# Latent attention and MLP on one core: first loads in finer pieces, low rotary passes on 64 rows, and the order of the attention pairs around them

## The reference

```python
def mla_mixer(x, w_in, q_norm, kv_norm, w_uq, w_ukv, w_o):
    h = x @ w_in                                   # 2048 -> 512 (q), 512 (kv), 64 (rotary key)
    cq, ckv = rms_norm(h[..., :512], q_norm), rms_norm(h[..., 512:1024], kv_norm)
    q = (cq @ w_uq).reshape(B, S, 16, 128 + 64)    # 128 plain and 64 rotary columns
    kv = (ckv @ w_ukv).reshape(B, S, 16, 128 + 128)
    q_rope, k_rope = apply_rope(q[..., 128:]), apply_rope(h[..., 1024:])   # one rotary key for all heads
    o = causal_softmax_attention(concat(q_nope, q_rope), concat(k_nope, k_rope), v, 192 ** -0.5)
    return o @ w_o

h = layer_norm(ALPHA * x + mla_mixer(x, ...))
out = layer_norm(ALPHA * h + jnp.square(jax.nn.relu(h @ w1)) @ w2)
```

## Time and profile before

| | us |
|---|---|
| median of three runs | 1808.7 |
| profiled execution | 1811.48 |
| its span, first to last instruction | 1809.5 |
| TensorE busy | 1784.0 |
| VectorE busy | 1533.6 |
| ScalarE busy | 942.4 |
| GpSimd busy | 175.0 |

### The profile page before, as it was taken

The page is one execution under the profiler, slowest core; times in us unless marked ns, Lnnn a source line. Parts: engine busy times, 40 slices in busy tenths (PEclk is TensorE's granted clock), DMA queues, the critical chain, the costliest instruction groups (busy, mean ns, idle before and its releaser), DMA issues.

```text
span 1809.5 us, 26333 instructions
## 1 busy us (share of the span) xinstructions
PE 1784.0 (99%) x9980; PEld 1555.3 (86%) x9980; DVE 1533.6 (85%) x1866; ACT 942.4 (52%) x1189; POOL 175.0 (10%) x98
## 2 busy tenths in 40 slices
PE   9999999999999999999999999999999999999997
PEld 7878988977889999999999999988888888888886
DVE  3167777699999999999999999989889999989986
ACT  4256666553456666666666666644333334333442
POOL 2333323000020000000000000000011111100003
PEclk9999999999999999999999999999999999999999
DMA  6222433598224766566556656678475474754832
GB/s 236 94 74 90 139 119 119 200 342 301 104 81 167 235 211 202 175 206 212 191 186 209 213 175 200 238 307 328 153 273 199 181 287 158 275 200 163 308 121 93
DMA packets 131588, 351.23 MB, mean 194 GB/s; under 512 B 7616, under 2 KB 80192, under 8 KB 113088
## 3 DMA queue, kind: packets, MB, share of 16 engines
q1 hardware_dynamic: 57120, 275.14, 41.4%
q10 hardware_dynamic: 74400, 75.26, 13.3%
HBM read 268.06 MB, written 82.31 MB: 194 GB/s over the span
## 4 chain that ended last, share of the span: by engine, by line
PE 91%; DVE 6%; issue 1%; DMA 1%; ACT 1%; ACTq 0%; DVEq 0%
PE bank L2234 24%; PE bank L2238 24%; PE bank L2239 24%; PE bank L2571 12%; PE bank L2575 6%; PE bank L2417 1%; DVE w_lo L1600 1%; DMA o_b<-out_weights 1%; PE bank L2409 0%; PE bank L2407 0%; DVE small L1555 0%; DMA first_raw<-weights 0%; DVE small L1710 0%; DVE up_both L1806 0%; PE bank L2332 0%
## 5 line engine op out<-in xcount | busy, mean ns | idle before, releaser
L1299 ACT ACTIVATE w_hi<-d_b 128x1024 fp32r<-128x1024 f32 x180 | 189.5, 1061 | 299.0 <-PE bank L2239 240.4
L2234 PE MATMUL bank<-w_hi,down_act 128*128 128x512 f32 x864 | 336.7, 390 | 0.4 <-issue 0.4
L2238 PE MATMUL bank<-w_lo,down_act 128*128 128x512 f32 x864 | 336.2, 389 | 0.0
L2239 PE MATMUL bank<-w_hi,down_act 128*128 128x512 f32 x864 | 336.2, 389 | 0.0
L2571 PE MATMUL bank<-up_both,w_hi 128*128 128x512 f32 x896 | 321.1, 397 | 0.0
L2234 PE MATMUL bank<-up_both,w_hi 128*128 128x256 f32 x912 | 258.2, 283 | 1.2 <-issue 1.0
L2238 PE MATMUL bank<-up_both,w_hi 128*128 128x256 f32 x912 | 258.0, 283 | 0.0
L2239 PE MATMUL bank<-up_both,w_lo 128*128 128x256 f32 x912 | 257.9, 283 | 0.0
L1970 DVE TENSOR_TENSOR w_lo<-d_b,w_hi 128x1024 fp32r<-128x1024 f32 x180 | 215.0, 1228 | 22.8 <-ACT w_hi L1299 22.8
L2575 PE MATMUL bank<-up_both,w_lo 128*128 128x256 f32 x896 | 233.3, 281 | 0.0
L1819 DVE TENSOR_TENSOR w_lo<-up_b,w_hi 128x1024 fp32r<-128x1024 f32 x180 | 217.1, 1219 | 10.1 <-ACT w_hi L1044 10.1
(11 more groups left out here) (233 smaller groups left out, 3217.5 us busy)
## 6 DMA issues: line engine op xcount, KB each, us to landing
up_b<-up_weights SPq DMA_DIRECT2D x128, 512.0 KB, 4.5
d_b<-down_weights SPq DMA_DIRECT2D x64, 1024.0 KB, 5.4
down_act<-acts_kept SPq DMA_DIRECT2D x56, 1024.0 KB, 5.3
acts_kept<-h_hi ACTq DMA_DIRECT2D x32, 896.0 KB, 4.2
acts_kept<-h_lo ACTq DMA_DIRECT2D x32, 896.0 KB, 5.5
raw<-weights SPq DMA_DIRECT2D x44, 512.0 KB, 3.3
o_b<-out_weights SPq DMA_DIRECT2D x16, 1024.0 KB, 8.5
o_act<-o_kept SPq DMA_DIRECT2D x13, 1024.0 KB, 9.4
```

The lines of the kernel that those rows point to most:

```text
L1299: act.activation(w_hi[:, DOWN_SLOT[n], :], source[:, ab, :], ACT.Copy).then_inc(down_hi, 1)
L2234: first_pass = pe.matmul(out_, a_hi, b_hi, start=start, stop=False, skip_group_check=more)
L2238: pe.matmul(out_, a_hi, b_lo, start=False, stop=False, skip_group_check=more)
L2239: return pe.matmul(out_, a_lo, b_hi, start=False, stop=stop, skip_group_check=more)
```

## The change

Sizes and loads. `kr_lo` has one copy of the low key in each half of the partitions instead of two half-empty ones, and is no longer filled with zeros. Of blocks 0 and 2, columns 0 to 255 and 256 to 511 come in pieces of 128 KB each on ScalarE's queue, and the last 512 columns in one piece each (block 0 on ScalarE's queue, block 2 on SyncE's, after x tile 3):

```diff
-            load_rest(1, 4)
             load_x_tile(3, 4)
+            sp.dma_start(first_raw[:, 1, 2 * FIRST_COLS:HB], w[2, :, 2 * FIRST_COLS:HB]).then_inc(first_loaded[11], 16)
...
-            for j in range(2):
-                act.dma_start(first_raw[:, j, 0:FIRST_COLS], w[2 * j, :, 0:FIRST_COLS]).then_inc(first_loaded[2 * j], 16)
-            act.dma_start(first_raw[:, 0, FIRST_COLS:HB], w[0, :, FIRST_COLS:HB]).then_inc(first_loaded[3], 16)
-
-            def first_weights(j):
-                act.wait_ge(*((first_loaded[0], 16), (first_loaded[2], 32))[j])
-                act.activation(w_hi[:, j, 0:FIRST_COLS], first_raw[:, j, 0:FIRST_COLS], ACT.Copy).then_inc(first_hi, 1)
+            for n in range(4):
+                j, cols = n % 2, slice(FIRST_COLS * (n // 2), FIRST_COLS * (n // 2) + FIRST_COLS)
+                act.dma_start(first_raw[:, j, cols], w[2 * j, :, cols]).then_inc(first_loaded[n + 1 if n else 0], 16)
+            act.dma_start(first_raw[:, 0, 2 * FIRST_COLS:HB], w[0, :, 2 * FIRST_COLS:HB]).then_inc(first_loaded[11], 16)
+
+            def first_weights(n):
+
+                j, cols = n % 2, slice(FIRST_COLS * (n // 2), FIRST_COLS * (n // 2) + FIRST_COLS)
+                act.wait_ge(first_loaded[n + 1 if n else 0], 32 if n else 16)
+                act.activation(w_hi[:, j, cols], first_raw[:, j, cols], ACT.Copy).then_inc(first_hi, 1)
```

The splits on ScalarE and VectorE follow: pieces 0 to 3 go ahead of the x tiles k = 0 to 3, the two remaining halves ahead of k = 4 and 5. On TensorE each of the three matmuls of k = 0 to 3 waits only for the parts that it reads:

```diff
+            def opening_product(j, k):
+
+
+                cols, n = slice(P * k, P * k + P), 2 * (k // 2) + j
+                pe.wait_ge(first_hi, n + 1)
+                pe.wait_ge(x_hi_made, k + 1)
+                pe.matmul(bank[:, j, :], w_hi[:, j, cols], act_hi[:, k, :], start=k == 0, stop=False)
+                pe.wait_ge(first_lo, n + 1)
+                pe.matmul(bank[:, j, :], w_lo[:, j, cols], act_hi[:, k, :], start=False, stop=False)
+                pe.wait_ge(x_split, k + 1)
+                pe.matmul(bank[:, j, :], w_hi[:, j, cols], act_lo[:, k, :], start=False, stop=False)
...
+            for k in range(4):
+                for j in range(2):
+                    opening_product(j, k)
+            for g in range(2, KD // 4):
```

Scores. The low rotary passes of both heads run together after all other passes, each on the 64 partitions of its head:

```diff
+                    product(score_block(h, t), q_hi[:, h, q], q_lo[:, h, q], k_hi[:, h, keys], k_lo[:, h, keys], t != 2, False, t == 2)
+
+                    pe.matmul(score_block(h, t), qr[:, h, q], kr_hi[:, keys], start=False, stop=False,
+                              skip_group_check=t == 2)
+
+            def score_lows():
+
+
+                for t in range(TT):
+                    q, keys = slice(P * t, P * t + P), slice(0, P * (t + 1))
+                    for half, h in zip(halves, range(2)):
+                        last = pe.matmul(score_block(h, t), qr[half, h, q], kr_lo[half, keys], start=False, stop=True,
+                                         skip_group_check=t == 2, tile_position=(64 * h, 0))
+                        if t == TT - 1:
+                            last.then_inc(scored, 1)
```

```diff
             root_of(1)
+            key_cross()
             weights(HB_QKV + 2)
-            key_cross()
-            weights(HB_QKV + 3)
             key_swap()
             latent_his(1)
+            weights(HB_QKV + 3)
...
-            def rope_query(pair, stream=True):
-                if stream:
-                    weights(HB_QKV + QKV_HB, pair)
+            def rope_query(pair):
                 rope_swap(pair + 1, rope_bank(pair))
 
-            def rope_query_hi(pair):
+            def rope_query_hi(pair, stream=True):
                 act.wait_ge(rope_rotated, pair + 2)
                 for half, h in zip(halves, range(2)):
                     last = act.activation(qr[half, h, :], rot[half, :], ACT.Copy)
                 last.then_inc(rope_hi, 1)
+                if stream:
+                    weights(HB_QKV + QKV_HB, pair)
...
+                if is_first(pair):
+                    act.activation(root[:, 0:1], ones[:, 0:1], ACT.Exp)
...
+                if behind:
+                    head_parts_lo(pair - 1)
                 maxima(pair, 0)
+                if ahead:
+                    query(pair + 1, 0)
                 maxima(pair, 1)
                 normalise(pair, 0)
                 if ahead:
-                    query(pair + 1, 0)
-                else:
-                    head_parts_lo(pair - 1)
+                    query(pair + 1, 1)
```

More of the change, by code:

```diff
@@ L187, in mla_mlp_program @@
         halves = (slice(0, 64), slice(64, 128))
-        kr_hi, kr_lo = sb("kr_hi", [P, S], f32r), sb("kr_lo", [P, 2, S], f32r)
-        place[0] += 2 * KB
+        kr_hi, kr_lo = sb("kr_hi", [P, S], f32r), sb("kr_lo", [P, S], f32r)
+        place[0] += 4 * KB
         v_hi, v_lo = sb("v_hi", [P, TT, 2 * VDIM], f32r), sb("v_lo", [P, TT, 2 * VDIM], f32r)
@@ L306, in score_diagonal @@
             return pairs.rearrange("p o (i n) -> p o i n", i=2)[:, :, :, 0:P]
-        first_loaded = [sem(f"first_loaded{g}") for g in range(11)]
+        first_loaded = [sem(f"first_loaded{g}") for g in range(12)]
         first_hi, first_lo = sem("first_hi"), sem("first_lo")
@@ L953, in attention @@
                     store_heads(pair - 1, 0)
+                if ahead:
+                    query(pair + 1, 0)
                 exps(pair, 0)
                 if ahead:
-                    query(pair + 1, 0)
+                    query(pair + 1, 1)
                 exps(pair, 1)
                 if ahead:
-                    query(pair + 1, 1)
-                    rope_query(pair + 1, stream)
+                    rope_query(pair + 1)
                 else:
@@ L965, in attention @@
                     key(pair + 1, 0)
-                    rope_query_hi(pair + 1)
+                    rope_query_hi(pair + 1, stream)
                 else:
@@ L1511, in key_rope_lo @@
             def key_rope_lo():
-                for h in range(2):
-                    last = dve.memset(kr_lo[64 - 64 * h:128 - 64 * h, h, :].bitcast(f32), 0.0)
-                last.then_inc(ones_made, 1)
                 dve.wait_ge(rope_hi, 1)
-                dve.wait_ge(ones_made, 2)
-                for half, h in zip(halves, range(2)):
-                    last = dve.tensor_tensor(kr_lo[half, h, :], rot[halves[0], :], kr_hi[halves[0], :].bitcast(f32), ALU.subtract)
+                for half in halves:
+                    last = dve.tensor_tensor(kr_lo[half, :], rot[halves[0], :], kr_hi[halves[0], :].bitcast(f32), ALU.subtract)
                 last.then_inc(rope_split, 1)
@@ L1648, in attention @@
                 if ahead:
-                    query(pair + 1, 0)
-                else:
-                    head_parts_lo(pair - 1)
+                    query(pair + 1, 1)
                 normalise(pair, 1)
                 if ahead:
-                    query(pair + 1, 1)
-                    if behind:
-                        head_parts_lo(pair - 1)
                     rope_query(pair + 1)
@@ L2294, in _ @@
                 pe.matmul(bank[:, 7, 0:P], ones[:, :], ones[:, :], start=True, stop=True)
-            for g in range(KD // 4):
+            for k in range(4):
+                for j in range(2):
+                    opening_product(j, k)
+            for g in range(2, KD // 4):
                 for j in range(2):
@@ L2403, in scores @@
                     q, keys = slice(P * t, P * t + P), slice(0, P * (t + 1))
-                    dst = score_bank(h)[:, SCORE_AT[t]:SCORE_AT[t] + P * (t + 1)]
-                    product(dst, q_hi[:, h, q], q_lo[:, h, q], k_hi[:, h, keys], k_lo[:, h, keys], True, False)
-                    pe.matmul(dst, qr[:, h, q], kr_hi[:, keys], start=False, stop=False)
-                    last = pe.matmul(dst, qr[:, h, q], kr_lo[:, h, keys], start=False, stop=True)
-                last.then_inc(scored, 1)
+                    product(score_block(h, t), q_hi[:, h, q], q_lo[:, h, q], k_hi[:, h, keys], k_lo[:, h, keys], t != 2, False, t == 2)
[9 more added lines that the diff above has]
+                            last.then_inc(scored, 1)
             def transpose_probs(pair, h):
@@ L2461, in attention @@
                 scores(pair, 1)
+                score_lows()
                 if ahead:
```

35 lines of the change are left out of this document (17 added, 18 removed).

## The result

The changed kernel takes 1820.34 us (median of 6 runs, 1819.84 to 1822.68), the kernel before 1808.74 beside it. The ratio is 1.0066, 95% interval 1.0053 to 1.0079. The forecast was 1805.4, in a range of 1802.5 to 1809.2, with a chance of 0.05 for slower. It was wrong in direction and size.

A forecast was written before the change was run, and what follows sets the result against it. TensorE, busy 1784.0 of 1809.5 us, was taken to bound the kernel. Opening -3.4, pair 0 0.0, pairs 1 to 6 -1.1, last pair +1.2 sum to -3.3: 1805.4 us from 1808.7, range 1802.5 to 1809.2.

The forecast's parts named there:

- The step that failed: Pairs: ScalarE waits for a weight load; head copies behind it are needed 1.9 us later, so no loss was counted.
- part 2: Pairs 1 to 6: low rotary passes on 64 rows and new order, 30.66 + L per pair, -1.1 us in all.
- The prediction's own sign of being wrong: Pairs less than 31.2 or more than 32.0, a further wait at head products, or pair 0 over 1 us off.
- Part 1, the opening: First stage: smaller pieces let x tile 3 come earlier, k=8 at 18.0 instead of 21.5; -3.4 us.
- rival A: Opening: the clock falls again in the gaps left, 1.5 us less is won, 1806.9; chance 0.27.
- L: Time of a pair's eight low rotary passes on 64 rows, switches included: 0.95 us, ends 0.84 and 2.8.
- eight loads one behind the other: Low rotary passes: loads costing by columns would make all eight load-bound, L near 1.05, the sum 0.6 us worse.
- with a margin of 0.1: Pairs: head 1's low probabilities are made at 26.6 us after the start, when TensorE arrives, so no wait.
- Part 3: Before and in pair 0: starts at 130.7 instead of 129.99, pair 1 at 163.1; 0.0 us, between -0.7 and +0.7.
- Part 4, the last pair: Last pair: no query tiles cover the later maxima, transposes start 2.2 later; +1.2 us (0 to +2).
- Slower: Whole kernel: a time above 1812.3 us, chance 0.05, made up of D and a little of another rival.
- D: Low rotary passes: weight loads not pulled ahead, L = 2.8, +10.0 in pairs 1 to 6, 1816.5; chance 0.04.

The follow-up runs named there:

- e3: Changed kernel with SyncE's first 4 MB of output projection loads held until pair 4's stores have landed too; 1809.30 us, ratio 0.9999.
- e2_store_early: Changed kernel with the store of o_lo issued directly behind ScalarE's second exponentials instead of behind the second key's weight blocks; 1810.01 us, ratio 1.0004.
- b1: Kernel before with only the opening's change (pieces, waits and `opening_product` of the first stage); 1807.32 us, ratio 0.9989.
- c3: c2 with, in the last pair, each head's low rotary passes directly behind that head's scores; 1807.31 us, ratio 0.9992.
- second profile of before: Kernel before, unchanged, profiled in one further execution; 1808.01 us, span 1806.2.
- c2: c1 with VectorE's low half of the query's rotary part behind head 1's low probabilities and the second key, in every pair; 1808.69 us, ratio 1.0002.
- c4: c3 with weight blocks 18 and 19 back in their old places ahead of the key's crossing and swap; 1805.35 us, ratio 0.9983.
- b2: b1 plus the low rotary passes on 64 rows behind both heads' scores, with ScalarE's and VectorE's order of before; 1820.65 us, ratio 1.0064.
- c1: e2_store_early with, in the last pair alone, VectorE's split of the previous pair's output back between the two normalisations; 1809.12 us, ratio 1.0005.

## Why the prediction was wrong

**The step that failed** stands in part 2: "ScalarE also waits for a weight load there, because the buffer is released later; behind it stand head copies that the next scores need 1.9 us later." The wait was seen; what is queued behind it was counted one short. Behind the block stands also the DMA issue of `store_heads(pair - 1, 1)`. By itself that is a wait of 0.45 us on ScalarE (e3). In pair 5 alone it puts the store into the 4 MB of SyncE, and the next pair waits for it: the rounding of the output, which stands at the head of ScalarE's order as before, and behind it the split, which the change had just put at the head of VectorE's. I had worked out one pair and multiplied by six; the pair in which another queue starts something new was the one to work out. Pair 6: +9.95, of which some 1.6 is the lower clock after the standstill (eight matmuls in 3.47, at 0.2275 they take 1.82). All three experiments that part the two transfers bring pair 6 to 31.7. The prediction's own sign of being wrong, a pair of more than 32.0, shows here. Without this step the result would still have missed the forecast: e2_store_early, which takes it away, has 1810.01, 4.6 more than forecast.

**Part 1, the opening (-3.4).** Against the first profile even -3.9: k=8 starts at 17.65 (18.0 forecast), the gaps left were 0.20 and 0.18, and the clock stayed at 1.00. The course of the opening was right, and rival A did not come. But it was measured against a single execution that ran 2.8 above the median, and I carried that distance to the result as if it lay outside the change. It lay in it: in the other two profiles of before k=8 starts at 19.13 and 19.17 instead of 21.56, without the half clock of the earlier trace rows and with x tile 3 copied 0.75 earlier. The term is worth 1.45 by the traces and 1.6 by b1's medians.

**Part 2, pairs 1 to 6 (-1.1).** L is 0.92 with the step into it, 0.95 forecast. The Trainium skill (TensorE: Matmul & The Clock Gate, LDWEIGHTS) has a weight load cost by its columns, not its rows, and the trace agrees: a load's record in pair 1 is 182 to 188 ns on 64 rows (`kr_lo`, changed kernel) and 187 to 192 on 128 (`kr_hi`, before). What the prediction made of it, eight loads one behind the other, is not so: in the changed kernel's trace the first loads of the two heads start at 164.841 and 164.844, and four passes (c3) take 0.83 where eight take 0.84. The Trainium skill (TensorEngine Tiling (Array Packing), Key Properties) has independent tiles and a drain at each switch of mode, which agrees with both numbers; that the remainder is drain no run here isolates. What was mis-sized is the waits. In pair 3, against the second profile of before, the first transposes start 0.17 late relative to the products ahead of them (0.13 forecast) and take 0.07 more, and the products of both heads take 3.97 instead of 3.77 (forecast none, "with a margin of 0.1"). So pairs take 31.88 where 31.6 was said. The last was the hold of GpSimd on qr, and c2 takes it away. The Trainium skill (SBUF — State Buffer; SBUF: two separate sides) says that a VectorE operation with two SBUF inputs and a GpSimd operation that reads SBUF lock each other out: qr is such a one, pt_lo has one of its two from PSUM, and the numbers of e2 and c2 agree.

**Part 3 (0.0).** The forecast was pair 0 starting 0.7 later and lasting 32.4 (130.7 to 163.1). Instead it starts unchanged: from the key's rotary tile to pair 0 the kernel before and the changed one both take 30.32 to 30.33. c4 and b2, without the zero fill and with the two blocks in their old places, take 29.07. So leaving out the fill is worth 1.25 with the blocks in their old places, and the late blocks ate exactly that, which is luck; the hold on the rotation was foreseen, that the two cancel was hidden in the sum of 0.0. Pair 0 itself is 0.5 to 0.65 longer, not shorter. The changed kernel's profile has the lower clock there (four matmuls of 0.63), but that is not the cause: in e3_loads_later the clock stays up and pair 0 takes 33.58. TensorE waits there for the bank of the values, which the kernel before doesn't:

```profile
133.79 0.50 PE L2235 MATMUL bank<-mid_hi,w_hi 128*128 128x512 f32 x1 [1.37 <-DVE v_lo L1525]
```

Which move of the new order brings this wait, no run isolates.

**Part 4, the last pair (+1.2).** +2.3. The transposes did start 2.2 later, as worked out (13.0 after the pair's start, give 10.8), but I took some of it to be made up; 2.3 stayed. The joint end of the scores is most of the cause: b2, with the old order, has the last product at 20.10 as c2 has, and c3 takes 1.5 off. The split's place is a little of it (0.27, c1), and so is the clock: c1 and c2 run the same program in the last pair and wait 2.31 ahead of the transposes, but c1 has the last product at 20.48 and c2 at 20.10. The six us around it, c1 from 363 and c2 from 362 (granted clock third from the end):

```profile
363.00:369.00 6.00, 5.65 (x28) 4.93 (x29) 5.96 (x10) 3.44 (x8) 0.00 (x0) 0.72 0.90 340
```

```profile
362.00:368.00 6.00, 4.66 (x29) 3.75 (x30) 5.96 (x11) 4.19 (x9) 0.00 (x0) 1.00 0.98 377
```

The changed kernel's profile has the lower clock there too (0.57 on the mean from 373 to 377).

**The chances.** Slower had 0.05, nearly all of it on one mechanism (D), which did not occur. A move of instructions on two engines and their queues deserved more for the chain not looked at.

## What to carry to other kernels

When an instruction that can wait is moved, list what its engine issues behind it, DMA issues above all, and for each who waits for its landing. Then look for the one iteration in which another queue begins a burst; a periodic sum hides it. Before pricing a stall from one profiled execution that is off the median, take a second profile: the stall may be what puts it off.

## What the runs showed of the hardware that I had not expected

- A store of 896 KB lands in 4.1 us when 4 MB of loads follow 4.1 us later (before), in 5.6 with a weight load of 512 KB beside it (e3), and in 16.4 when the 4 MB are issued on another queue in the same microsecond (changed).
- The same program has different clocks in its first 17 us from execution to execution. Between 6 and 17 us the three profiles of before have half rate in 6.3 to 9.9, in 13.2 to 16.6, or not at all. Half rate early cost nothing (k=8 starts at 19.13, against 19.17 without it), since TensorE then waited less for the loads; half rate late cost about 1.7 us, half of the time that it lasted (an estimate).
- After the same wait of 2.31 us in the last pair the clock fell in c1's profile and stayed up in c2's. The fall cost 0.4 us there, because TensorE had later waits that took up the rest.
- Four matmul passes on 64 rows, alone between passes on 128, take 0.83 us (c3), the undivided four 0.64 (before), and eight on both halves 0.84 (changed): dividing one product alone loses.
